# Constants multiplied in TensorE's waits, and the mixer's output projection begun inside the last attention items

## What is computed

```python
for l in range(DEPTH):
    h = h + 0.5 * rms_norm(swiglu(rms_norm(h, g[0]), gate1, up1, down1), g[1])
    m = hybrid_mixer(rms_norm(h, g[2]), w_in, w_out)
    h = h + rms_norm(m, g[3])
    h = h + 0.5 * rms_norm(swiglu(rms_norm(h, g[4]), gate2, up2, down2), g[5])
```

## Time and profile before

| | |
|---|---|
| median of 3 runs | 2077.1 us |
| the profiled execution | 2078.51 us |
| its span in the trace | 2076.7 us |
| TensorE busy | 94% of the span |
| mean granted TensorE clock | 0.97 of full speed |
| FFN 1 / mixer / FFN 2 of layer 0 (first matmul to first matmul) | 30 to 424 / 424 to 671 / 671 to 1045 us |
| the same of layer 1 | 1045 to 1437 / 1437 to 1685 / 1685 to 2062 us |

### The profile page before, as it was taken

One profiled execution on the slowest core, in us unless ns is written; L12 is line 12 of the kernel. 1 busy time (PEld: TensorE's weight loads), 2 busy tenths in 40 slices (PEclk: granted clock), 3 DMA queues, 4 the chain that ended last, 5 costly groups with the idle time before them and its releaser, 6 DMA issues.

```text
span 2076.7 us, 24925 instructions
## 1 busy us (share of the span) xinstructions
PE 1961.5 (94%) x8954; PEld 1570.1 (76%) x8954; DVE 1127.0 (54%) x1597; ACT 880.5 (42%) x1398; POOL 209.3 (10%) x409
## 2 busy tenths in 40 slices
PE   5999999999888999999999999999988899999996
PEld 4777888877657788888877788887865677888885
DVE  3674553376655755552377645425865566555323
ACT  4544442254553554441254444323555445445221
POOL 6502000012100000000057010000220000000000
PEclk8999999999999999999999999999989999999998
DMA  5324343252112233343232343333411123333321
GB/s 156 88 85 122 103 117 97 64 147 77 51 31 81 63 100 101 92 117 98 82 95 85 106 115 112 99 93 86 152 32 31 52 81 91 101 92 112 98 84 41
DMA packets 330426, 188.51 MB, mean 91 GB/s; under 512 B 6981, under 2 KB 325417, under 8 KB 329321
## 3 DMA queue, kind: packets, MB, share of 16 engines
q1 hardware_dynamic: 324520, 168.65, 28.2%
q0 software_dynamic: 5824, 18.79, 3.0%
HBM read 175.72 MB, written 11.67 MB: 90 GB/s over the span
## 4 chain that ended last, share of the span: by engine, by line
PE 74%; DVE 13%; ACT 9%; issue 3%; DMA 0%; SPq 0%; DVEq 0%; ACTq 0%
PE ps L496 13%; PE ps L498 12%; PE ps L497 12%; PE ps L639 8%; PE ps L641 8%; PE ps L640 8%; DVE wl L1333 4%; ACT wh L907 2%; PE ps L540 1%; PE ps L541 1%; PE ps L545 1%; PE ps L788 1%; DVE hT L1394 1%; PE ps L737 1%; ACT sig L987 1%
## 5 line engine op out<-in xcount | busy, mean ns | idle before, releaser
L1333 DVE TENSOR_TENSOR wl<-raw,wh 128x1024 fp32r<-128x1024 f32 (+1 forms) x272 | 358.7, 1319 | 534.1 <-ACT wh L907 533.0
L496 PE MATMUL ps<-xh,wh 128*128 128x512 f32 x1536 | 607.4, 395 | 11.8 <-DVE wl L1333 11.8
L497 PE MATMUL ps<-xl,wh 128*128 128x512 f32 x1536 | 601.3, 391 | 0.0
L498 PE MATMUL ps<-xh,wl 128*128 128x512 f32 x1536 | 601.2, 391 | 0.0
L907 ACT ACTIVATE wh<-raw 128x1024 fp32r<-128x1024 f32 (+1 forms) x272 | 307.0, 1130 | 463.1 <-PE ps L641 341.4
L496 PEld LDWEIGHTS ps<-xh,wh 128*128 128x128 f32 x1536 | 290.9, 189 | 78.8 <-DVE wl L1333 16.8
L498 PEld LDWEIGHTS ps<-xh,wl 128*128 128x128 f32 x1536 | 290.5, 189 | 61.6
L497 PEld LDWEIGHTS ps<-xl,wh 128*128 128x128 f32 x1536 | 291.0, 189 | 59.4
L639 PE MATMUL ps<-Hh,wh 128*128 128x512 f32 x704 | 278.3, 395 | 0.0
L641 PE MATMUL ps<-Hh,wl 128*128 128x512 f32 x704 | 277.9, 395 | 0.0
L640 PE MATMUL ps<-Hl,wh 128*128 128x512 f32 x704 | 277.8, 395 | 0.0
(11 more groups left out here) (296 smaller groups left out, 2116.9 us busy)
## 6 DMA issues: line engine op xcount, KB each, us to landing
raw<-in_ffn_gate SPq DMA_DIRECT2D x88, 512.0 KB, 3.9
raw<-in_ffn_up SPq DMA_DIRECT2D x88, 512.0 KB, 3.8
raw<-in_ffn_down SPq DMA_DIRECT2D x64, 704.0 KB, 4.5
raw<-in_w_in SPq DMA_DIRECT2D x28, 512.0 KB, 4.1
raw<-in_w_out SPq DMA_DIRECT2D x16, 512.0 KB, 3.7
yF<-in_x SPq DMA_DIRECT2D x1, 2048.0 KB, 9.2
ssm_t<-evict POOLq DMA_DIRECT2D x8, 256.0 KB, 4.3
ssm_v<-evict POOLq DMA_DIRECT2D x8, 256.0 KB, 2.7
```

The lines of the kernel that those rows point to most:

```text
L496: pe.matmul(bank, w_tile(True, slot, kw), xh[:, kx, :], start=first, stop=False)
L497: pe.matmul(bank, w_tile(True, slot, kw), xl[:, kx, :], start=False, stop=False)
L498: return pe.matmul(bank, w_tile(False, slot, kw), xh[:, kx, :], start=False, stop=last)
L1333: V.tensor_tensor(w_low(slot, k0, nk), raw[:, slot4, 0:nk - k0, :], w_high(slot, k0, nk).bitcast(F32), ALU.subtract).then_inc(w_split, 1)
```

## The change

`spin(bank, count)` multiplies the constant `identb` with the constant `maskb` (128x384, bf16) `count` times into a bank that nobody reads before it is written anew. It stands behind `post_norm` of all six stages but the last (18 matmuls) and in step 3 of the mixer (12 matmuls, between the scores and the turn). In the output projection four banks take part (`out_bank`): units 0 and 1 go to banks 6 and 1, and their tiles 0 to 5 are multiplied in steps 26 to 29, 31 and 32 (`OUT_AT`), six matmuls each. Units 2 and 3 follow after the items, then the rest. The splits of units 0 to 3 are in steps 21, 22, 30 and 31 on ScalarE and one step later on VectorE; unit 3's goes to the slot over `qa`. Units 4 and 5 are split ahead of the first `square_out`.

```diff
 def out_slot(i):
-    return (1, 0, X_ROT)[i] if i < 3 else i % 2
+    return (1, 0, X_ROT, X_QA)[i] if i < 4 else i % 2
+def out_bank(d):
+    return (6, 1, 2, 3, 4, 5, 2, 3)[d]
...
+            def spin(bank, count):
+                for _ in range(count):
+                    pe.matmul(ps[bank][:, 0:3 * P], identb[:, :], maskb[:, :], start=True, stop=True, skip_group_check=True)
...
+                if dn + KD < DEPTH * 3 * KD:
+                    spin(PRE_BANK, SPIN_HOLE)
...
+                def out_part(d0, ks):
+                    n = l * U_LAYER + U_OUT + d0
+                    for k in ks:
+                        if k == 0:
+                            pe.wait_ge(w_split, n + 1 + RAW_SLOTS + 1)
+                            if d0 == 0:
+                                pe.wait_ge(proj_free[1], (l + 1) * len(IN_BANK1) + 1)
+                                pe.wait_ge(br_r, l * 3 + 1)
+                            else:
+                                pe.wait_ge(s_exp, (l + 1) * N_ITEMS)
+                        pe.wait_ge(x_rdy, (l * 4 + 2) * KD + k + 1)
+                        for d in (d0, d0 + 1):
+                            mm = three(ps[out_bank(d)][:, :], out_slot(d), k, k, k == 0, k == KD - 1)
+                            if k == KD - 1:
+                                mm.then_inc(unit_done, 1)
...
+                    if s in SPIN_AT:
+                        spin(BU_BANK[0], SPIN_AT[s])
                     if LAG_T <= s < N_ITEMS + LAG_T:
                         turn(s - LAG_T)
...
+                    if s in OUT_AT:
+                        out_part(0, OUT_AT[s])
...
-                pe.wait_ge(y_used, l * (3 * KD) + KD + 2)
-                slots = [out_slot(i) for i in range(2)]
-                first_two(n, OUT, l * 4 + 2, range(0, 3), slots)
+                out_part(2, range(0, 3))
                 fox_sum(7)
-                first_two(n, OUT, l * 4 + 2, range(3, KD), slots)
-                out_four(0, 2, out_slot)
-                out_four(1, 0, lambda i: out_slot(4 + i))
+                out_part(2, range(3, 6))
+                out_part(0, range(6, KD))
+                out_part(2, range(6, KD))
+                for d in range(4, KD):
+                    if d >= 6:
+                        pe.wait_ge(y_used, l * (3 * KD) + KD + d - 1)
+                    unit_x(l * U_LAYER + U_OUT + d, out_slot(d), ps[out_bank(d)][:, :])
                 post_norm(l * (3 * KD) + KD)
...
-                    if s == 30:
-                        for i in range(3):
-                            split_unit(l * U_LAYER + U_OUT + i, out_slot(i), KD, 4 if i == 2 else 2)
+                    if s in OUT_SPLIT_AT:
+                        i = OUT_SPLIT_AT[s]
+                        split_unit(l * U_LAYER + U_OUT + i, out_slot(i), KD, (2, 2, 4, 5)[i])
...
-                    if s_ == 31:
-                        for i in range(3):
-                            low_unit(l * U_LAYER + U_OUT + i, out_slot(i))
+                    if s_ - 1 in OUT_SPLIT_AT:
+                        i = OUT_SPLIT_AT[s_ - 1]
+                        low_unit(l * U_LAYER + U_OUT + i, out_slot(i))
...
+SPLIT_BEHIND = {0: (4, 5), 4: (6,), 5: (7,)}
+OUT_SPLIT_AT = {21: 0, 22: 1, 30: 2, 31: 3}
+OUT_AT = {26: (0,), 27: (1,), 28: (2,), 29: (3,), 31: (4,), 32: (5,)}
+SPIN_HOLE, SPIN_AT = 18, {3: 12}
```

More of the change, by code:

```diff
@@ L286, in build @@
         BU_BANK, POST_BANK, PRE_BANK = (6, 7), 6, 7
-        DOWN, OUT = (4, 5), (2, 3)
+        DOWN = (4, 5)
         GLU_BANK = (5, 7)
@@ L505, in unit_x @@
                 mm.then_inc(unit_done, 1)
[L507 to L524, removed]
             def first_four(cols, xn, s):
@@ L850, in mixer @@
                         glu()
-                n = l * U_LAYER + U_OUT
-                pe.wait_ge(y_used, l * (3 * KD) + KD + 2)
-                slots = [out_slot(i) for i in range(2)]
-                first_two(n, OUT, l * 4 + 2, range(0, 3), slots)
+                out_part(2, range(0, 3))
                 fox_sum(7)
-                first_two(n, OUT, l * 4 + 2, range(3, KD), slots)
[L858 to L862, removed]
-                out_four(0, 2, out_slot)
-                out_four(1, 0, lambda i: out_slot(4 + i))
+                out_part(2, range(3, 6))
[5 more added lines that the diff above has]
+                    unit_x(l * U_LAYER + U_OUT + d, out_slot(d), ps[out_bank(d)][:, :])
                 post_norm(l * (3 * KD) + KD)
@@ L1211, in mixer @@
                 x_high(7)
[L1213 to L1224, removed]
+                n = l * U_LAYER + U_OUT
+                for d in range(KD):
+                    for i in SPLIT_BEHIND.get(d, ()):
+                        split_unit(n + i, out_slot(i), KD, {4: 3, 5: 5}.get(i, 2))
+                    if d == 7:
                         split_ahead(l * 3 + 2, 0)
                         split_ahead(l * 3 + 2, 1)
-                    square_out(l * (3 * KD) + KD + 4 + i, l * U_LAYER + U_OUT + 4 + i, OUT[i % 2])
+                    square_out(l * (3 * KD) + KD + d, n + d, out_bank(d))
             act.wait_ge(prm_rdy, 1)
@@ L1769, in mixer @@
                 x_tile_low(7)
[L1771 to L1781, removed]
+                for d in range(KD - 1):
+                    for i in SPLIT_BEHIND.get(d, ()):
+                        low_unit(l * U_LAYER + U_OUT + i, out_slot(i))
+                    out_tile(l, l * (3 * KD) + KD + d, yM[:, d, :], d, 1.0, out_bank(d), 3, d == 0)
                 low_ahead(l * 3 + 2, 0)
                 low_ahead(l * 3 + 2, 1)
-                out_last(l, l * (3 * KD) + KD + 7, yM[:, 7, :], 7, 1.0, OUT[1], 3)
+                out_last(l, l * (3 * KD) + KD + 7, yM[:, 7, :], 7, 1.0, out_bank(7), 3)
             for i in range(4):
```

## The result

The changed kernel takes 2056.0 us (median; 2054.0 to 2059.3), the kernel before 2077.3 us beside it: a ratio of 0.9899, 95% interval 0.9881 to 0.9916. The profiled execution took 2057.3 us, its span is 2055.5 us.

A forecast was written before the change was run, and what follows sets the result against it. TensorE, busy 94%, was taken as the bound, with time to win only in its waits and lowered clock; 2078.5 - 0.9 - 5.9 - 15.3 + 3.1 + 3.4 = 2062.9, less 1.4 for the median: 2061.5 us, range 2052 to 2070.

The forecast's parts named there:

- Boundaries, -0.9: Constants behind `post_norm`: 0.5 us saved at each mixer-to-FFN-2 boundary, nothing at the other three; -0.9 us in all.
- Step 3, -5.9: Constants ahead of the mixer's turn: `ssm_out` falls to 3.8 us, saving 3.3 + 2.65 us; -5.9 us in all.
- the 3.9 us behind it: Further saving on work behind `ssm_out` if the clock stayed up through it, 1.55 + 2.35 us; left out.
- My rival with the clock up: Neither `ssm_out` (-3.9) nor the hole of step 24 (-3.4) lowers the clock: 2054.2 us, chance 0.22.
- Output projection inside the items, -15.3: Moved matmuls, last items and output projection: 11.6 us of waits and 5.75 us of clock saved, less 2.0 us.
- the 2.0 us for insertions: Cost of twelve insertions among the items, 0.15 us each, with 0.2 us for short waits in the tail.
- Earlier splits, +3.1 and +3.4: Branch sum of step 24: hole grows by 1.55 us per layer (+3.1); lower clock behind it, 1.7 per layer (+3.4).
- Constants don't hold the clock: Rival: bf16, mostly zero constants leave the clock down, only the output projection pays: 2068.3 us, chance 0.12.
- The items absorb less: Rival: added work or longer chains in the items leave some 6 us won instead of 15.3: 2070.8 us, chance 0.12.
- The slower rival: Constants outlast their holes and delay TensorE's queue: 2083 us at half clock, 2100 us with unhidden weight loads; chance 0.04.
- the unhidden weight load: Rival: at full clock each constant takes 0.269 us because its load isn't hidden, adding 6.7 us: 2068 us, chance 0.05.
- The signs: Right if `first_four` waits under 1 us, clock 1.00, `ssm_out` under 4 us, `pre_norm` over 1 us, step 24 2.6 us.

The follow-up runs named there:

- third kernel: The kernel before with only the eighteen constant matmuls behind `post_norm` at the stage boundaries added: 2076.6 us, ratio 0.9999.
- step 3 alone: The kernel before with only the twelve constant matmuls in step 3 of the mixer added: 2070.1 us, ratio 0.9958.

## Why the prediction came out as it did

The forecast was 2061.5 us, in a range of 2052 to 2070; measured were 2056.0 us. The sign, the range and the order of the parts held. Step 3 and the output projection gave more than forecast, the earlier splits cost more; that these cancel in part is luck.

**Boundaries, -0.9: right** (-1.1, within what these two boundaries vary by themselves: 26.5 us each in the kernel without constants). The reading that the added squares end last (692.90 against 693.39) was the whole point. The third kernel shows it: clock up at five boundaries, five waits of 1.0 us at `pre_norm` in exchange, no measurable gain. Where a wait on `pre_norm` shows up even at the lower clock, the clock is worth nothing there.

**Step 3, -5.9: mis-sized** (-10.3 in the profile, 10.0 with that part alone). `ssm_out` came to 3.79 us, the 3.8 us taken from `ssm_direct`. The step that failed is the choice to leave out the 3.9 us behind it. I had read "the clock did not rise during `ssm_out`" as "it may fall during `ssm_out`". Every kernel with the constants ahead of it has 1.00 in it, and every one without them 0.50. My rival with the clock up had this half right.

**Output projection inside the items, -15.3: close, for partly other reasons.** At full clock the stretch takes 65.0 us, 17.0 us less than before for both layers (73.3 + 73.8 - 2 x 65.0), close to the 11.6 us of waits and 5.75 us of clock. The size of the parts was near as well: per layer 3.1 us for the spread splits and the banks, 2.6 us for the place of the matmuls. But I had put the waits for the last norms down to the three low parts in a row; with the splits spread and the matmuls behind the items, 2.9 of their 3.9 us are still there, so it is the moved matmuls that fill them. Most of the waits for turned probabilities (2.6 of 3.4 us) went with the splits and banks, not with the moved matmuls.

The term that was mis-sized is the 2.0 us for insertions. I had written that the trace has no such switch, but the kernel before has it at every late projection, whose matmuls stand between the matmuls of an item. First the start of such a group in the kernel before, then of one of the moved groups in the kernel with constants in the sums:

```profile
509.85 0.47 PE L496 MATMUL ps<-xh,wh 128*128 128x512 f32 x1
510.17 0.39 PE L497 MATMUL ps<-xl,wh 128*128 128x512 f32 x1
...
591.88 0.50 PE L501 MATMUL ps<-xh,wh 128*128 128x512 f32 x1
592.21 0.39 PE L502 MATMUL ps<-xl,wh 128*128 128x512 f32 x1
```

From the first to the second matmul it is 0.32 and 0.33 us in place of 0.23, so some 0.1 us per insertion, 1.2 us for twelve. The balance, 11.6 + 5.75 - 1.2 against 17.0, leaves some 0.8 us without a place.

**Earlier splits, +3.1 and +3.4: right in place, the first too high as a wait, the second too low.** The wait of step 24 grew by 1.1 and 1.0 us, less than my 1.55. The stretch between the sums grew by 3.7 us all the same, because in layer 0 the clock stood at 0.50 behind step 21 for 6.4 us in place of 3.3, some 1.5 us that no term had. The fall behind step 24 came in both layers of the profiled execution and cost 68.2 - 65.0 = 3.2 us each, 6.3 us instead of 3.4. In other kernels' executions with a wait of 2.0 to 2.2 us there, it came (the matmuls behind the items, both layers) or didn't (30 constants, layer 0). It is thus a cost that varies between executions.

The sum of the terms as measured is -1.1 - 10.3 - 17.0 + 6.3 + 3.7 = -18.4, and the untouched first stage had 3.1 us less in this profile: -21.2 with the +0.3 of the rest. My terms made -15.6: 4.4 us of the difference are step 3, 1.7 us the projection, against them 3.5 us that the earlier splits cost above my terms. The rest of the 5.5 us between forecast and measurement is about the untouched first stage.

**The rivals.** "Constants don't hold the clock" fell with step 3 alone. "The items absorb less" fell: from step 26 there is no wait of 0.5 us. The slower rival needed 0.29 us per constant and the unhidden weight load 0.269 us; measured are 0.163 us, below the 0.171 us scaled from the projection's matmuls.
The Trainium skill (TensorE: Matmul & The Clock Gate, "Part 3: Packing small matmuls — row/col tiling") says that a weight load overlaps running matmuls only if it goes to other rows of the array. The trace doesn't agree for these matmuls, which use all rows: 27 loads were busy for 2.65 us of 4.40 us in which the matmuls left no gap.

**The signs.** The waits of `first_four` (0.9 us), the clock of 1.00 behind the constants, `ssm_out` (3.79 us) and the waits from step 26 on came as named. The wait on `pre_norm` grew to 1.0 us, not over it, and the sum of step 24 waits 2.2 and 2.0 us, not 2.6.

What stays open: the separate gains of constants and output projection fall short of the whole by some 4 to 5 us, in the medians and in the profiled spans (8.8, 6.0 and 1.9 us against 21.2). 2.2 us of this are the time that step 3 alone loses again behind step 21; the untouched stretches vary by as much as the rest. Where in an execution the clock falls was seen to differ from one to the next; what decides it was not tried.

## What to carry to other kernels

A wait of TensorE has two prices, its own length and the work behind it at half clock; the second can be the larger, and matmuls of constants in the wait removed it for nothing here, where they all started at full clock and another engine set the end of the wait. Before doing so at a place, look whether TensorE's cold work is what ends last there: at the stage boundaries it was not. And when work is moved ahead, look at what it is put in front of on the other engines: one low part of 1.2 us, one step too early on VectorE, cost 2.2 us between the sums of the two layers, and some 5 us of 2056 with the fall of the clock behind it (by medians whose intervals overlap).

## What the runs showed of the hardware

What stands ahead of a stretch can decide its clock throughout. `ssm_out`'s matmuls (64 rows, 63 columns, in pairs) ran at 0.50 to their end in all three kernels without constants ahead of them, 6.8 us in layer 0 of the kernel before, and the clock rose only among the split 512-column matmuls of a late input projection behind them. With constants ahead of them they ran at 1.00 without its falling, 3.79 us.

The items' matmuls (66 to 128 rows, 64 to 512 columns, float32, with short waits between) held a clock of 1.00 over all last items in one kernel. They also run while it comes back, but after very different times: 6.9 us in one layer of the kernel with the matmuls behind the items, 16.7 us in the other, TensorE busy all the time. Nor does the length of a wait alone decide whether the clock falls: behind the same wait of 2.2 us at step 24 it fell in layer 0 of the changed kernel and not in layer 0 of the kernel with 30 constants, and it fell behind 1.6 us in layer 1 of that one.

Constants in bf16, one operand an identity, hold the clock: twelve of them ahead of `ssm_out`, 0.163 us apart, with their weight loads beside them.
